# Results of even groups stored below partition 64, of odd groups above it

## The reference, cut to what matters

```python
n = 2 * L
y = jnp.fft.irfft(jnp.fft.rfft(s, n=n, axis=1) * jnp.fft.rfft(g, n=n, axis=0)[None],
                  n=n, axis=1)[:, :L]
y = (y + s * skip.astype(jnp.float32)).astype(u.dtype) * x0
return y @ w_out + b_out
```

## Time and profile before

| | |
|---|---|
| median of three runs | 2460.16 us (2460.12 to 2461.47) |
| the profiled execution's own time | 2460.01 us |
| its span | 2458.2 us |
| mean granted TensorE clock | 0.984 |
| busy: TensorE, VectorE, ScalarE, GpSimd | 96%, 45%, 25%, 26% |
| DMA | 211.51 MB, mean 86 GB/s |

### The profile page before, as it was taken

One profiled execution on the slowest core, in us unless ns is written; L12 is line 12 of the kernel. 1 busy time (PEld: TensorE's weight loads), 2 busy tenths in 40 slices (PEclk: granted clock), 3 DMA queues, 4 the chain that ended last, 5 costly groups with the idle time before them and its releaser, 6 DMA issues.

```text
span 2458.2 us, 29269 instructions
## 1 busy us (share of the span) xinstructions
PE 2365.6 (96%) x11692; PEld 1900.3 (77%) x11692; DVE 1107.8 (45%) x1131; ACT 605.4 (25%) x672; POOL 646.3 (26%) x362
## 2 busy tenths in 40 slices
PE   7999998799999999999997999999999999999996
PEld 5766772378888888888886888989897877778885
DVE  6765445352662055413366827363543024500533
ACT  4333313422110010001123626262633011111011
POOL 2221210123333233333342122222222233323321
PEclk9999999899999999999998999999999999999997
DMA  4143239512221223112111202020214221112231
GB/s 155 51 124 127 89 123 342 208 35 84 96 85 43 85 77 102 51 43 69 51 59 36 103 27 77 26 77 26 77 33 172 102 77 56 56 43 67 96 120 68
DMA packets 75331, 211.51 MB, mean 86 GB/s; under 512 B 22006, under 2 KB 25912, under 8 KB 75002
## 3 DMA queue, kind: packets, MB, share of 16 engines
q1 hardware_dynamic: 64794, 172.72, 21.5%
q10 hardware_dynamic: 10464, 37.75, 4.1%
HBM read 165.36 MB, written 40.37 MB: 84 GB/s over the span
## 4 chain that ended last, share of the span: by engine, by line
PE 75%; DVE 3%; ACT 1%; issue 0%; ACTq 0%; DVEq 0%
PE ps L1205 63%; PE ps L538 5%; DVE T L1855 1%; PE ps L1479 1%; PE ps L585 1%; PE ps L604 1%; PE ps L605 1%; PE ps L567 1%; PE ps L606 1%; PE ps L1227 1%; DVE XN L1885 0%; PE ps L1236 0%; PE ps L504 0%; DVE X L2179 0%; DVE H L1878 0%; PE ps L523 0%
## 5 line engine op out<-in xcount | busy, mean ns | idle before, releaser
L1205 PE MATMUL ps<-H,whi 128*128 128x512 f32 x4000 | 1083.9, 393 | 20.6 <-DVE H L1922 10.1
L1205 PEld LDWEIGHTS ps<-H,whi 128*128 128x128 f32 x4000 | 750.9, 189 | 198.1 <-issue 28.9
L1155 POOL CAST whi<-wraw 128x1024 fp32r<-128x1024 f32 x174 | 182.3, 1048 | 1690.4 <-PE ps L1205 842.8
L1205 PE MATMUL ps<-H,wlo 128*128 128x512 f32 x2000 | 618.2, 390 | 0.0
L1157 POOL TENSOR_TENSOR wlo<-wraw,whi 128x1024 fp32r<-128x1024 f32 x178 | 452.2, 2540 | 53.2 <-ACT whi L672 39.3
L1205 PEld LDWEIGHTS ps<-H,wlo 128*128 128x128 f32 x2000 | 376.8, 188 | 79.3
L1205 PE MATMUL ps<-A,whi 128*128 128x512 f32 x1472 | 395.8, 391 | 9.3 <-DVE A L2211 4.9
L1205 PEld LDWEIGHTS ps<-A,whi 128*128 128x128 f32 x1472 | 276.9, 188 | 68.3 <-issue 5.3
L1205 PE MATMUL ps<-A,wlo 128*128 128x512 f32 x736 | 227.4, 390 | 0.0
L1205 PEld LDWEIGHTS ps<-A,wlo 128*128 128x128 f32 x736 | 138.7, 188 | 29.0
L2095 DVE TENSOR_TENSOR T<-ps,T 128x1024 f32<-128x1024 f32 x22 | 26.9, 1224 | 155.8 <-PE ps L1205 155.8
(11 more groups left out here) (336 smaller groups left out, 2307.3 us busy)
## 6 DMA issues: line engine op xcount, KB each, us to landing
wraw<-in_panels SPq DMA_DIRECT2D x181, 512.0 KB, 3.6
mw<-in_modp SPq DMA_DIRECT2D x24, 512.0 KB, 3.6
g<-gsp SPq DMA_DIRECT2D x16, 512.0 KB, 3.7
gr<-g SPq DMA_DIRECT2D x16, 512.0 KB, 12.6
bs<-s SPq DMA_DIRECT2D x16, 512.0 KB, 12.2
YB<-yi ACTq DMA_DIRECT2D x16, 512.0 KB
X<-in_xT SPq DMA_DIRECT2D x4, 1024.0 KB, 7.1
s<-sa SPq DMA_DIRECT2D x8, 512.0 KB, 2.7
```

The lines of the kernel that those rows point to most:

```text
L1155: nc.gpsimd.tensor_copy(whi[:, s, :, :], wraw[:, s, :, :]).then_inc(hi_made, 1)
L1205: last = mm(p[:, c * step:(c + 1) * step], w[:, ws, k, :], operand(act, a, k, c * step, step), start=(q == 0 and w is whi and a == 0), sto ...
```

## The change

The partitions of `YB` to which a group's result goes are others: even groups go to the partitions 0 to 63, odd groups to 64 to 127, each still to every fourth of a window of 32. Groups 0, 2, 4, 6 take the window 0 to 31; 8, 10, 12, 14 take 32 to 63; 1, 3, 5, 7 take 64 to 95; 9, 11, 13, 15 take 96 to 127. The rows of `idft` are loaded in the matching order, again by four DMAs. The buffers, the issuing engine, the sizes and every wait stay.

```diff
         def y_rows(g):
-            return slice(g % 4 + 32 * (g // 4), g % 4 + 32 * (g // 4) + 29, 4)
+            b = 64 * (g % 2) + 32 * (g // 8) + g // 2 % 4
+            return slice(b, b + 29, 4)
...
-            for a in range(0, P, 32):
-                sp.dma_start(cst[a:a + 32, CST["idft"]:CST["idft"] + HALF],
-                             d["cst"][a:a + 32, CST["idft"]:CST["idft"] + HALF].rearrange("(b r) c -> r b c", r=8)
+            rows = d["cst"][:, CST["idft"]:CST["idft"] + HALF].rearrange("(w b s r) c -> s w r b c", w=2, b=4, s=2)
+            for q in range(4):
+                sp.dma_start(cst[32 * q:32 * q + 32, CST["idft"]:CST["idft"] + HALF], rows[q // 2, q % 2, :, :, :]
                              ).then_inc(const_in, 16)
```

## The result

The changed kernel takes 2466.01 us (median of 17 runs, 2459.63 to 2468.01), the kernel before, in as many runs beside it, 2460.84 us (2458.79 to 2466.53). The ratio is 1.0017, with a 95% interval of 1.0010 to 1.0025: it is slower by some 4.2 us. The profiled execution took 2466.77 us with a span of 2465.0.

The account below looks back on a forecast made before the run. The prediction took eight DMA engines, carrying both loads and stores, to bound the spectral stage. Two more collisions at 1.4 us gave +2.8 on 2460.01, so 2462.8 us, tail taken as nothing; range 2453.5 to 2468.5 us.

Parts of the forecast that it names:

- The bound: Spectral stage: the eight engines carrying loads and stores have 6.2 us of work per group, the other eight 3.7.
- theory 2: Follow-up expectation for the spectral stage: GpSimd's stores alternate between two sets of eight engines; fuller engines' work 5.0 us a group.
- rival (b): Spectral stage: engines follow the destination, upper stores use the other eight, pace falls to 5.0 us; about 2445.6 us, chance 0.07.
- A count, not a balance: Spectral stage: upper stores collide beside loads; two freed, four new, so two more collisions, +2.8 us.
- The price of a collision: Stores above partition 64 beside loads: a loaded engine's work rises from 6.2 to 7.6 us, so 1.4 us each.
- The upper bound of 2.7 us: Late spectral stage, highest price of one collision: the whole loss of pace, 8.6 - 5.9 us a group.
- Rival (a): Late spectral stage: successive upper stores build up pressure, alternating dissolves the collision; two steps fall to 5.9 us; 2454.0 us, chance 0.18.
- `idft` and the rest of the program: Early loads of `idft`: the new order costs nothing, four DMAs of 8.0 KB then as now.
- The tail: Last stores, without loads beside them: taken as nothing, with -2.1 us kept as an end; wait stays near 9.67 us.
- Rival (c): Early spectral stage: collisions beside the densest loads cost the full 2.7 us each; 2465.4 to 2468.4 us, chance 0.28.
- (d): Spectral stage: no effect, late stretch slow from memory reads or collisions making up for another; 2460.0 us, chance 0.15.
- The signs to look for: Spectral stage: early store packets 165 to 170 ns, late ones below 185, steps more even, last result 2 to 3 us later.

Follow-up runs that it names:

- The run on the tail: Against the kernel before, the stores of groups 12 to 15 take their data from the signal rows in device memory instead of `yi`; 2458.84 us, ratio 0.9993.

## Why the prediction was right, and where it was off

- **The bound.** That eight engines carry the stores and set the pace was the step everything rests on. It held: while the changed kernel waits in its longest step, both queues together hold 51.9% of the engines (448 to 451 us); and with GpSimd issuing, by theory 2 from two sets of engines in turn and each in its own place, the stage came down to 4.8 us a group. I had estimated 5.0 for this case in rival (b) and in the expectation.
- **A count, not a balance.** Held. Balanced use of the halves made it slower; a shift of four partitions within one half made it slower too. Counting stores that go up while loads run, relative to the kernel before: -3 gives -5.9 us, +2 gives +4.2, +5 gives +10.6, +8 gives +12.1. The store of group 11 is left out of these counts; in the changed kernel it goes up beside a load, but with packets of 156 ns.
- **The price of a collision was probably too small.** I took 1.4 us, the extra work of a loaded engine. The ratios give 5.9 / 3 = 2.0, 4.2 / 2 = 2.1, 10.6 / 5 = 2.1 and 12.1 / 8 = 1.5. Divided in the same way, their intervals are 1.1 to 2.7, 1.2 to 3.1, 1.3 to 2.9 and 1.0 to 2.0: each of them still holds 1.4. So the sign and the count were borne out by four runs, the size is only known to lie between 1 and 3 us.
- **What the price is made of stays open.** Part of it is the clock. The length of a stretch times what is missing to full clock comes to 3.4 us in the kernel before, to nothing with all stores below 64, to 6.9 with the halves exchanged and to 7.8 with all above (366 to 449.2 us). At most 3.4 of the 5.9 us, 3.5 of the 10.6 and 4.4 of the 12.1 are of that kind, following the longer gaps. Part may be that a late load is felt more than its own delay: three sets of buffers tie loading to computing, so a stall of TensorE makes the next loads start late as well. The steps of 8.3 and 9.5 us followed by three of 4.3 look like this; it is my reading, no run took it apart. And ScalarE's waits for a store, 3.9 and 3.7 us with the early stores up, were no term of my sum.
- **The upper bound of 2.7 us was badly read.** I took two steps of 8.6 us each from group 9 to group 11. By the same rows they were 5.9 (423.81 to 429.67) and 11.3 (429.67 to 440.96): one long gap, with the granted clock at 0.79 around it, not a pace. Rival (a), which lets "the two late steps" fall, used the same mean.
- **`idft` and the rest of the program.** Nothing to see, as forecast, except 1.1 us before the first result, in one profiled execution each. The run on the tail, whose kernel differs from the one before only from group 12 on, has its first result at 378.60, 0.8 us later than before, so this is mostly spread. The runs' own spread (2458.79 to 2466.53 for the kernel before) is wider than that.
- **The tail** was set at nothing, and is: 9.14 against 9.67 us of waiting, and the same slow packets whichever half is written.
- **Rival (a)**, a dissolving collision, fell: packets were longer in the early stretch (176 ns), and the late one had 189, not less than 185 as I had written. The stage being later, that window now holds the store of 7, that of 8, which goes down, and 90 of the 136 packets of that of 9 (952 packets are through at 424.7, 1314 at 441). **Rival (c)** is not parted from my forecast by the time: its +5.4 and my +2.8 both lie within the interval of the ratio, 2.5 to 6.2 us, and the median of 2466.01 even lies in its range (2465.4 to 2468.4) and above the upper end of my sum (2465.4). The denser early loads did make longer packets (213 and 223 ns in the two runs with all early stores up, against 185 late), as it says; only the run with all stores above 64, with at most 2.0 us a collision, speaks against its price. That the time fell into my range owes as much to the width of the range, which was made to take in (c), as to the sum. **Rival (b)**, engines that follow the destination, is wrong for ScalarE's queue: exchanging halves would have been free. **(d)** is out with the interval above 1.
- **The signs to look for.** I had said 165 to 170 ns (it was 176), a load's packet above 137 (146), in the late stretch a load's below 166 (153) and a store's below 185 (189, a miss), a last result 2 to 3 us later (6.5, of which 5.4 belong to the stage), and steps more even than before. The last of these was wrong too: they are less even.
- **The clock.** The granted clock fell in two stretches of the stage, 0.83 at 416 to 424.7 and 0.82 at 441 to 449.2, where before it fell in one, 0.79 at 424.7 to 441. The length times what is missing to full clock is 8.7 x 0.17 + 8.2 x 0.18 = 3.0 us now, and 16.3 x 0.21 = 3.4 before: about the same. Here the clock doesn't explain the difference.

## What to carry to other kernels

The store with 8 destination partitions holds 47.4% of the engines when it is alone, so eight of them, and beside other transfers it is these engines, not the mean share of all sixteen, that set the pace: look at what share a queue holds when it is alone. Then ask for each destination which engines write there in the transfers that run beside it, and put the part that must go to foreign partitions where nothing else runs. A balance over partitions helps only if the engines alternate with it; here that took another issuing engine, and the same partitions were then worth -12 us instead of +4.

## What the runs showed of the hardware

- Four partitions matter: with the early stores moved up by four partitions (4 to 35 instead of 0 to 31, and so on), a packet takes 175 instead of 152 ns beside loads, in one profiled execution, and the kernel 5.4 us more, in ten.
- A store above partition 64 takes 213 to 223 ns a packet beside dense loads, and 156 ns where both queues together hold about eight engines' worth (448 to 451 us of the changed kernel).
- Which partitions are good depends on the issuing engine: with GpSimd, exchanging even and odd groups is worth 19 us (2448.65 against 2468.00). That it decides which DMA engines carry a store is inferred from this, for no row names an engine.
- With GpSimd issuing, a load costs 40 us of engine time per MB in the one order of halves and 60 in the other; the bytes are the same. With ScalarE issuing and the early stores below 64 it is 45.9.
- Alone, stores within SBUF on eight engines are slower (215 ns a packet, 222 with all stores below 64) than beside loads (152). Why is open.
